# Moving the decay logs of the gated attention into the input projection, and one conditioning chunk out of the attention's head

## What is computed

```python
mod = silu(c) @ w_ada + b_ada                      # six parts of 1024, for 9 conditioning rows
h = rms_norm(x) * (1 + sc1) + sh1
q_sb, k_sb, v_sb, q_g, k_g, v_g, r_g, a_low = split_columns(h @ w_in)     # a_low is 16 wide
log_a = log_sigmoid(a_low @ w_gla_gate + b_gla_gate) / 16                  # 256 wide
b = cumsum(log_a) within a chunk
# scores = tril((q*exp(b)) @ (k*exp(-b))), o = scores @ v + (q*exp(b)) @ state
o_g = rms_norm(o) * silu(r_g)
x = x + ga1 * (concat([o_sb, o_g]) @ w_out)
x = x + ga2 * (square(relu(h2 @ w_up)) @ w_down)   # h2: normed and modulated with sc2, sh2
```

## Time and profile before

| | |
|---|---|
| median of 3 runs | 1842.41 us (1842.07 to 1846.49) |
| the profiled execution | 1845.04 us |
| its span, first to last instruction | 1843.4 us |
| mean granted TensorE clock | 0.945 |
| PE busy | 1678.4 us (91%) |
| DVE, ACT, POOL busy | 736.4, 604.0, 433.8 us |
| gated attention, from its first DMA to DVE's last instruction | 745.2 to 915.3 us of the span |

### The profile page before, as it was taken

The page is one execution under the profiler, slowest core; times in us unless marked ns, Lnnn a source line. Parts: engine busy times, 40 slices in busy tenths (PEclk is TensorE's granted clock), DMA queues, the critical chain, the costliest instruction groups (busy, mean ns, idle before and its releaser), DMA issues. The chain is left out here.

```text
span 1843.4 us, 27703 instructions
## 1 busy us (share of the span) xinstructions
PE 1678.4 (91%) x10864; PEld 1462.3 (79%) x10864; DVE 736.4 (40%) x1252; ACT 604.0 (33%) x1138; POOL 433.8 (24%) x306
## 2 busy tenths in 40 slices
PE   5999996999968888687589899999999999999997
PEld 2899994777744444265479799999999999999997
DVE  3501003444457778446803543232333232323225
ACT  3511102323357778335334431212121211112123
POOL 0022204222200000200144542323333232323230
PEclk8999996999989999577789999999999999999999
DMA  9133117666220000843162221111101111111102
GB/s 326 47 120 125 55 46 234 204 207 195 83 104 23 24 1 1 261 151 107 43 234 92 92 69 47 46 46 35 49 29 46 46 46 46 46 46 46 46 12 98
DMA packets 116177, 164.54 MB, mean 89 GB/s; under 512 B 6970, under 2 KB 80141, under 8 KB 116086
## 3 DMA queue, kind: packets, MB, share of 16 engines
q1 hardware_dynamic: 110864, 146.49, 24.4%
q0 software_dynamic: 5120, 16.78, 2.9%
q10 hardware_dynamic: 102, 0.03, 0.0%
HBM read 141.98 MB, written 21.30 MB: 89 GB/s over the span
## 5 line engine op out<-in xcount | busy, mean ns | idle before, releaser
L468 PE MATMUL psum<-op_hi,out_hi 128*128 128x384 f32 (+1 forms) x960 | 320.7, 334 | 3.7 <-DVEq L2557 2.0
L470 PE MATMUL psum<-op_hi,out_lo 128*128 128x384 f32 (+1 forms) x960 | 314.4, 327 | 0.0
L469 PE MATMUL psum<-op_lo,out_hi 128*128 128x384 f32 (+1 forms) x960 | 314.3, 327 | 0.0
L468 PE MATMUL psum<-mlp_a_hi,out_hi 128*128 128x384 f32 (+1 forms) x768 | 251.0, 327 | 0.5 <-DVE x1T L2584 0.5
L470 PE MATMUL psum<-mlp_a_hi,out_lo 128*128 128x384 f32 (+1 forms) x768 | 250.8, 327 | 0.0
L469 PE MATMUL psum<-mlp_a_lo,out_hi 128*128 128x384 f32 (+1 forms) x768 | 250.5, 326 | 0.0
L2474 POOL TENSOR_TENSOR out_lo<-out_raw,out_hi 128x2048 fp32r<-128x2048 f32 x31 | 143.2, 4621 | 271.6 <-ACT out_hi L2497 271.6
L2570 DVE TENSOR_TENSOR mlp_sq<-mlp_relu 128x384 f32<-128x384 f32 (+1 forms) x96 | 88.3, 921 | 280.4 <-ACT mlp_relu L2512 280.4
L468 PEld LDWEIGHTS psum<-op_hi,out_hi 128*128 128x128 f32 x960 | 181.5, 189 | 7.9 <-DVEq L2557 2.9
L469 PEld LDWEIGHTS psum<-op_lo,out_hi 128*128 128x128 f32 x960 | 181.5, 189 | 2.5
L470 PEld LDWEIGHTS psum<-op_hi,out_lo 128*128 128x128 f32 x960 | 181.3, 189 | 0.0
(11 more groups left out here) (338 smaller groups left out, 2999.1 us busy)
## 6 DMA issues: line engine op xcount, KB each, us to landing
sa_k<-in_cache_k SPq DMA_DIRECT2D x64, 256.0 KB, 3.1
sa_v<-in_cache_v POOLq DMA_DIRECT2D x64, 256.0 KB, 3.9
out_raw<-in_w_up SPq DMA_DIRECT2D x16, 1024.0 KB, 5.4
out_raw<-in_w_down SPq DMA_DIRECT2D x16, 1024.0 KB, 4.9
out_raw<-in_w_out SPq DMA_DIRECT2D x12, 1024.0 KB, 4.8
ada_w<-in_w_ada SPq DMA_DIRECT2D x22, 512.0 KB, 4.7
in_raw<-in_w_in SPq DMA_DIRECT2D x8, 1024.0 KB, 6.0
ada_w<-in_w_ada SPq DMA_DIRECT2D x3, 2048.0 KB, 13.8
```

Of the source, the lines that this page charges most:

```text
L468: pe.matmul(out, w_hi, x_hi, start=(k == 0), stop=False)
L469: pe.matmul(out, w_hi, x_lo, start=False, stop=False)
L470: return pe.matmul(out, w_lo, x_hi, start=False, stop=(k == nk - 1))
```

## The change

The bias, the logarithm and the scan move into `stage_project_in`. The last feature panel now forms only the 16 columns of `a_low` (the weights have 16 columns in place of 128, the streamed tokens are the same), which stay in SBUF in `stg[0]`; their store is gone. After groups 36 to 41 PE does one gate product each into the two spare banks, ACT and DVE do the rest between the groups that follow in the space of the stored k, and SP stores the result, 1088 KB, in the new DRAM tensor `logdecay`. The gated attention loads that in place of `a_low` and `w_gla_gate`, ahead of k and q, and its first steps are gone on PE, ACT, DVE and POOL.

`PRE` becomes 3. In the head only the first six quarters are loaded at once; the sample v, the states and r tile 0 stand ahead of quarters 6 and 7, and quarters 6 and above use the two slots. The third chunk ahead (`ada(2)`) stands behind `output(0)`, next to `ada(3)`, in round 0; the loop's chunks 4 to 7 stand in rounds 1 to 4, where before chunks 4 to 7 stood in rounds 0 to 3. Two of the initial turns of chunk rows move behind their chunk. DVE takes chunks 0, 1 and 2 in round 0 and chunks 3 to 7 in rounds 1 to 5.

```diff
         self.projT = nc.dram_tensor("projT", [IN_W, T], F32, kind="Internal").ap()
+        self.logdecay = nc.dram_tensor("logdecay", [P, 2, T], F32, kind="Internal").ap()
         self.vgnat = nc.dram_tensor("vgnat", [T, GH * GV], F32, kind="Internal").ap()
...
+    GATES = [(m, c) for m in range(2) for c in range(3)]
+    GATE_AT = NF + N9
...
+        nx, bc = (free[:, i * 2 * T:(i + 1) * 2 * T].rearrange("p (m t) -> p m t", m=2) for i in range(2))
+        reset = stg[1]
+        wg = g.sb("in_gate_w", [RANK, GH * GK], ctx=ctx)
+        negb = g.sb("in_gate_negb", [P, 2], ctx=ctx)
...
+                sp.dma_start(wg[:], io["w_gla_gate"][0]).then_inc(s_wg, 16)
...
-                        store_feature(8)
...
+                sp.wait_ge(s_gd, 4)
+                sp.dma_start(g.logdecay, bc).then_inc(s_go, 16)
                 evacuated(sp, len(groups))
...
+                    if p == V0 + 1:
+                        pool.wait_ge(s_out[1], 32)
+                        pool.wait_ge(s_kt, 6)
+                        pool.memset(reset[:], 1.0).then_inc(s_rs, 1)
+                        pool.wait_ge(s_rs, 1)
+                        pool.memset(reset[:, 0:TP:P], 0.0).then_inc(s_rs, 1)
+                        pool.memset(reset[:, TP:T:NEW], 0.0).then_inc(s_rs, 1)
...
-                            cols = slice(m * P, (m + 1) * P)
-                            last = three_products(pe, bank[:, 0:tw], w.hi[p % 2][:, k, cols], w.lo[p % 2][:, k, cols],
+                            cols = slice(m * P, (m + 1) * P) if p != AP else slice(P - RANK, P)
+                            last = three_products(pe, bank[0:cols.stop - cols.start, 0:tw], w.hi[p % 2][:, k, cols], w.lo[p % 2][:, k, cols],
...
+                    u = j - GATE_AT
+                    if 0 <= u < len(GATES):
+                        m, c = GATES[u]
+                        t0, tw = CHUNKS[c]
+                        if u == 0:
+                            evacuated(pe, NF)
+                            pe.wait_ge(s_wg, 16)
+                            pe.wait_ge(s_kc[0], NU // 2)
+                            pe.wait_ge(s_kc[1], NU // 2)
+                        at_least(pe, s_ga, u - 1)
+                        pe.matmul(g.bank[NB + u % 2][:, 0:tw], wg[:, m * P:(m + 1) * P], stg[0][0:RANK, t0:t0 + tw],
+                                  start=True, stop=True).then_inc(s_gp, 1)
...
+                def gate(u):
+                    if u == -1:
+                        dve.tensor_scalar(negb[:], g.vecT[:, 16:18], -1.0, None, ALU.mult).then_inc(s_gd, 1)
+                    if u == 10:
+                        dve.wait_ge(s_ga, 9)
+                        dve.scalar_tensor_tensor(out=flat(nx), in0=flat(nx), scalar=0.0, in1=flat(bc), op0=ALU.max,
+                                                 op1=ALU.add).then_inc(s_gd, 1)
+                    if u in (12, 14):
+                        m = (u - 12) // 2
+                        dve.wait_ge(s_rs, 3)
+                        dve.wait_ge(s_gd, 2)
+                        dve.tensor_tensor_scan(bc[:, m, :], reset[:], nx[:, m, :], 0.0, ALU.mult, ALU.add).then_inc(s_gd, 1)
+
...
+                    if 0 <= u - 1 < len(GATES):
+                        m, c = GATES[u - 1]
+                        t0, tw = CHUNKS[c]
+                        if u == 1:
+                            act.wait_ge(s_ko, 32)
+                            act.wait_ge(s_gd, 1)
+                        act.wait_ge(s_gp, u)
+                        act.activation(nx[:, m, t0:t0 + tw], g.bank[NB + (u - 1) % 2][:, 0:tw], ACT.Identity, scale=-1.0,
+                                       bias=negb[:, m:m + 1]).then_inc(s_ga, 1)
+                    if u == 7:
+                        act.wait_ge(s_ga, 6)
+                        act.activation(bc, nx, ACT.Abs).then_inc(s_ga, 1)
+                    if u == 8:
+                        act.wait_ge(s_ga, 7)
+                        act.activation(bc, bc, ACT.Exp, scale=-1.0).then_inc(s_ga, 1)
+                    if u == 9:
+                        act.wait_ge(s_ga, 8)
+                        act.activation(bc, bc, ACT.Ln, bias=1.0).then_inc(s_ga, 1)
...
-        al, wg = bc[0:RANK, 0, :], bc[0:RANK, 1, 0:GH * GK]
...
-        PRE = 4
+        PRE = 3
         PAIR_AT = {5: 0, 6: 1, 7: 2, 8: 3}
-        SLOT = [t % 6 if t < 4 * PRE else t % 2 for t in range(4 * NADA)]
+        SLOT = [t if t < 6 else t % 2 for t in range(4 * NADA)]
...
-        ADA = [g.bank[b] for b in (7, 6, 5, 4, 7, 7, 7, 7)]
+        ADA = [g.bank[b] for b in (7, 6, 5, 7, 7, 7, 7, 7)]
...
-                sp.dma_start(al, g.projT[ROW_A:IN_W, :]).then_inc(s_gin, 16)
-                sp.dma_start(wg, io["w_gla_gate"][0]).then_inc(s_gin, 16)
+                sp.dma_start(bc[:], g.logdecay).then_inc(s_gin, 16)
                 sp.dma_start(k[:], g.projT[ROW_KG:ROW_VG, :].rearrange("(m p) t -> p m t", p=P)).then_inc(s_k, 16)
                 sp.dma_start(q[:], g.projT[ROW_QG:ROW_KG, :].rearrange("(m p) t -> p m t", p=P)).then_inc(s_q, 16)
...
-                for i in range(4 * PRE):
+                for i in range(6):
                     weights(i)
                 sp.dma_start(vs[:], g.vgnat[tile(NT)]).then_inc(s_vs, 16)
-                sp.wait_ge(s_z, 4)
+                sp.wait_ge(s_z, 1)
                 s0d = io["state_gla"][0].rearrange("s (m h) k v -> h m k s v", h=2)
                 for h in range(2):
                     for m in range(2):
                         sp.dma_start(s0[HALF[h], :, 2 * m + h, :], s0d[h, m]).then_inc(s_s0, 16)
                 load_r(0)
+                weights(6)
+                weights(7)
                 load_v(0)
                 load_r(1)
                 load_v(1)
+                for i in range(8, 4 * PRE):
+                    weights(i)
...
-                act.wait_ge(s_nb, 1)
-                n = 0
-                for m in range(2):
-                    for c, (t0, tw) in enumerate(CHUNKS):
-                        act.wait_ge(s_gate, 3 * m + c + 1)
-                        act.activation(nx[:, m, t0:t0 + tw], g.bank[3 * m + c][:, 0:tw], ACT.Identity, scale=-1.0,
-                                       bias=negb[:, m:m + 1]).then_inc(s_a, 1)
-                act.wait_ge(s_a, 6)
-                act.activation(bc[:], nx[:], ACT.Abs).then_inc(s_a, 1)
-                act.wait_ge(s_a, 7)
-                act.activation(bc[:], bc[:], ACT.Exp, scale=-1.0).then_inc(s_a, 1)
-                act.wait_ge(s_a, 8)
-                act.activation(bc[:], bc[:], ACT.Ln, bias=1.0).then_inc(s_a, 1)
-
...
+                copy_kn(0)
                 ada_rows(1)
-                copy_kn(0)
-                ada_rows(2)
-                ada_rows(3)
                 for n in range(N9):
...
+                    if n == 0:
+                        ada_rows(2)
                     if n + PRE < NADA:
                         ada_rows(n + PRE)
...
-                dve.tensor_scalar(negb[:], g.vecT[:, 16:18], -1.0, None, ALU.mult).then_inc(s_nb, 1)
-                dve.wait_ge(s_a, 9)
-                dve.wait_ge(s_c, 7)
-                pre(dve.scalar_tensor_tensor(out=nx[:].rearrange("k m t -> k (m t)"), in0=nx[:].rearrange("k m t -> k (m t)"),
-                                             scalar=0.0, in1=bc[:].rearrange("k m t -> k (m t)"), op0=ALU.max, op1=ALU.add))
-                dve.wait_ge(s_d, 1)
-                for m in range(2):
-                    pre(dve.tensor_tensor_scan(bc[:, m, :], reset, nx[:, m, :], 0.0, ALU.mult, ALU.add))
-                dve.wait_ge(s_d, 3)
+                dve.wait_ge(s_gin, 16)
...
-                    for i in {0: (0, 1, 2, 3), 1: (4,), 2: (5,), 3: (6,), 4: (7,)}.get(n, ()):
+                    for i in {0: (0, 1, 2), 1: (3,), 2: (4,), 3: (5,), 4: (6,), 5: (7,)}.get(n, ()):
                         ada_mod(i)
-                    if n == 4:
+                    if n == 5:
                         scale_gain(dve, g, g.mul2, SC2, KD)
...
-                pe.wait_ge(s_gin, 32)
-                for m in range(2):
-                    for c, (t0, tw) in enumerate(CHUNKS):
-                        pe.matmul(g.bank[3 * m + c][:, 0:tw], wg[:, m * P:(m + 1) * P], al[:, t0:t0 + tw],
-                                  start=True, stop=True).then_inc(s_gate, 1)
-
...
-                for i in range(PRE):
-                    ada(i)
-                turn_ada(0)
-                pe.wait_ge(s_d, 13)
+                ada(0)
+                pe.wait_ge(s_d, 10)
                 turn_keys(0)
                 score(0)
-                for i in range(1, PRE):
-                    turn_ada(i)
+                turn_ada(0)
+                ada(1)
                 turn_keys(1)
                 score(1)
+                turn_ada(1)
                 for n in range(N9):
                     output(n)
+                    if n == 0:
+                        ada(2)
                     if n > 0:
                         outer(n - 1)
                         turn_out(n - 1)
...
```

(52 more changed lines are left out.)

16 lines of the change are left out of this document (1 added, 15 removed).

## The result

The change makes the kernel slower. The median of four runs is 1859.03 us (1857.91 to 1862.33), beside 1842.24 us for the kernel before in the same session (1839.87 to 1846.49): a ratio of 1.0082, 95% interval 1.0063 to 1.0100, so between 11.6 and 18.4 us. The forecast of 1854.4 us has the right sign, and 1859.03 lies within its range, 4.6 us above it. The profiled execution took 1859.53 us with a span of 1857.9 us, 14.5 us more than the span before.

A forecast was written before the change was run, and what follows sets the result against it. PE bounds the kernel, its head waiting for quarters' DMAs and the decay path; DVE bounds from about tile 5. Terms +4.3, -11.5, +13.2, +3.9, +2.1 make 12.0 us: 1842.41 to 1854.4 us, range 1843 to 1862.

The forecast's parts named there:

- What bounds the head: Head of the gated attention: 16 quarters' DMAs and DVE's decay path must both end; the change starts `output(0)` 11.5 us earlier.
- Input projection, +4.3: Input projection: six gate products at full clock cost 3.8 us, plus 0.5 us for changes of matmul kind.
- 0.5 us for six changes between the two kinds of matmul: Input projection: allowance on PE for switching between gate products and the other matmuls, 0.5 us in all.
- by other than 4 to 5 us: Sign of being wrong: the input projection grows by an amount outside 4 to 5 us.
- The states at the rate of the row: Head: the states' 1 MB in 512-byte rows loads at 185 GB/s, 5.7 us, delaying quarters 6 and 7.
- Round 0, 13.2 given back: Round 0, behind `output(0)`: two chunks and a turn give back 13.2 us, leaving `output(1)` 1.7 us later.
- from a release to the use it takes 3.9 us: Round 0, second chunk: each quarter is used 3.9 us after its slot is released.
- One more round with a chunk, +3.9: Loop: four rounds carry a chunk instead of three, at 15.1 us each against 11.1 without: +3.9 us.
- The tail, +2.1: After the loop: the last chunk's bias in round 5 delays tile 4's gate on DVE, +2.1 us, 7.7 in all.
- (a): TensorE's full clock from about 776 and faster transfers give 13.2 us: sum -1.2 us, median 1841.2 us; chance 0.12.
- (b): Later rounds: the fourth round with a chunk is hidden; sum 7.3 us, median 1849.7 us; chance 0.14.
- (c): Round 0 and the new round: 0.8 us more for each of eight uncovered quarters; sum 18.4, median 1860.8 us; chance 0.14.

The follow-up runs named there:

- logs_only: Kernel before with the logs made in the input projection and all four chunks kept in the head: 1853.36 us, ratio 1.0052.
- chunk_only: Kernel before with only the chunk leaving the head, gate products staying in the gated attention: 1860.35 us, ratio 1.0081.
- quarters_first: Kernel after with quarters 6 and 7 loaded ahead of the samples' v and states: 1853.06 us, ratio 1.0057.
- slots_after: Kernel after with four more slots for the later chunks' quarters, in operand tiles filled only by the last four tiles: 1824.6 us, ratio 0.9906.

## Why the prediction was right, and where it was off

- **What bounds the head.** Right: two bounds of one length. `logs_only` and `chunk_only` take away one each and get -1.0 and 3.9 us for it; together they get 12.1, where 11.5 was foretold. Of the 3.9 some 2.4 are the clock, which the account of the bounds had at 0.50.
- **Input projection, +4.3.** Off: 6.03 us. The failed term is the "0.5 us for six changes between the two kinds of matmul". A break costs 0.39 us, six cost 2.3; the products themselves cost 0.64 each, 3.8 in all, as the sum had it. 3.8 + 2.3 = 6.1, and 6.03 was measured. The place for "0.6 to 0.8 us" was 1.03. Growth "by other than 4 to 5 us" was one of the prediction's own signs of being wrong, and it came.
- **The states at the rate of the row.** Right in the time, not in the reason. Quarters 6 and 7 were foretold at 28.4 and 29.9 us after the first DMA (773.6 and 775.1 less 745.2) and came at 28.3 and 29.7; that it is so close is in part luck, since the first quarter was used at 12.0 us and not 12.9. The Trainium skill (DMA: Bandwidth & Descriptors, Specifications), with transfers of 512 bytes at line rate, would have had them 2.8 us earlier (2.6 by the 342 GB/s of the earlier trace rows). For the states this trace goes with the row of 185 GB/s. But their rows of 512 bytes are not the reason, as the sum and the expectation of `quarters_first` have it. Two windows of the kernel after, first the states, then r of tile 2 (128x4x128, issued at 801.06), whose rows have 512 bytes too:

```profile
772.00:775.00 3.00, 2.94 (x20) 2.38 (x24) 2.94 (x7) 0.27 (x2) 0.00 (x0) 0.50 1.20 195
804.50:805.00 0.50, 0.04 (x4) 0.00 (x0) 0.00 (x0) 0.00 (x0) 0.00 (x0) 0.88 1.12 340
```

  340 GB/s agrees with the page. The two loads differ otherwise: a DMA of the states fills 64 partitions and one of r fills 128, and they come from different tensors. Which of these makes the 195 was not tried.
- **Round 0, 13.2 given back.** Right in kind: of the head's 12.1 us nothing is left at `output(1)`. Short by 1.9 us in size, and this is the step of the loop that failed. From `output(0)` to `output(1)` 31.6 us were foretold (782.1 to 813.7) and 33.5 measured. The term is "from a release to the use it takes 3.9 us": it was read off the third quarter of the round and used for all, though the fourth had taken 4.85 us in the same rows. The first took 3.7 us, the three behind it 4.8. The fourth chunk took 11.9 us, and not 9.9, and the two together 18.9 and not 17.
- **One more round with a chunk, +3.9.** Measured +2.0 between `output(1)` and `output(5)` (5.0 less 3.0): rounds of 14.6 us on average and not 15.1. The two errors of the loop cancel, and that `output(5)` is within 0.6 us is luck.
- **The tail, +2.1.** Measured +1.3 to the gate of tile 4 and +2.3 to the last gate, 7.3 in all where 7.7 was foretold. DVE is the bound there, as said.
- **What is left.** Stage and projection make 13.3 of the 14.5 us of the two spans. Another 1.1 us lies between the last store and the first work of the next stage: 6.39 us after, 5.27 before. The eight kernels of the experiments, with the one or the other projection, have 5.2 to 5.8, so I take it for scatter from run to run; no run tests it. The median moved 16.8 us and not 14.5, inside what its interval allows.
- **The rivals.** (a) did not come: the clock stood at 0.50 until `output(0)` and at 0.70 during it. `quarters_first` and `chunk_only` show its clock to be real behind another order; in `chunk_only` the kernel was 0.8% slower than before all the same. (b) fell: the later rounds hide nothing, 7.3 us reach the last gate. (c) was right in part: trips of 4.8 us in round 0, but no longer rounds afterwards. Its 1860.8 us lies nearest to the median, by the projection's 1.7 us and the scatter between the stages, and not by its own mechanism, which gave 1.9 us and not 6.4.

The price of the slot was seen in the sum, but only as a term. That it was worth more than all that the change moved (31 us in `slots_after`) was not.

Not tried: quarters 6 and 7 held back by something other than the states, which would tell what the clock hangs on; logs made without any product in the projection's stream, and loads of the late quarters in larger pieces.

## What to carry to other kernels

Where two chains end a stage together, price the place that the moved work goes to, not the one that it leaves: here the head had a quarter every 1.5 us, and round 0 behind it a quarter every 3 us for want of slots. Look first for the wait "for a load that could not be issued", by comparing each load's issue with the release of its buffer; memory that other stages own but do not use at that time was the cure here. And an odd matmul put into a stream of another kind cost its own time and a break of 0.39 us here, so try to put such matmuls side by side.
